# The sums of the gate weights in the second block, made by accumulating transfers begun on GpSimd

## What is computed

```python
h = rmsnorm_2(x, pre_norm_g[l])
proj = h @ w_in[l]
(u, v, z_a, c_q, c_kv, k_rope, z_b, x_c, z_c, g_a, g_b, g_c) = jnp.split(proj, cuts, axis=-1)
y_a = gmlp_spatial(u, v, ...) * silu(z_a)
y_b = mla_attention(c_q, c_kv, k_rope, ...) * silu(z_b)
y_c = rg_lru(x_c, ...) * silu(z_c)
merged = (sigmoid(g_a) * (y_a @ w_proj_a[l]) + sigmoid(g_b) * (y_b @ w_proj_b[l])
          + sigmoid(g_c) * (y_c @ w_proj_c[l]))
x = x + rmsnorm_2(merged @ w_out[l], post_norm_g[l])
```

## Time and profile before

| | |
|---|---|
| median of 3 runs | 3142.86 us (3142.70 to 3143.12) |
| profiled execution, its own time | 3142.73 us |
| its span, first to last instruction | 3141.4 us |
| PE busy | 3129.8 us, 100% of the span |
| PEld busy | 2644.8 us, 84% |
| DVE busy | 1953.5 us, 62% |
| ACT busy | 1316.9 us, 42% |
| POOL busy | 546.5 us, 17% |
| POOL's 64 additions for the sums (L2530) | 1.31 to 1.39 us each, 2.30 at most |
| moved by DMA | 353.71 MB, 113 GB/s |

### The profile page before, as it was taken

How to read it: one execution, slowest core, us unless ns; L and a number is a source line. 1 busy time by engine, 2 the same in 40 slices (tenths; PEclk the granted TensorE clock), 3 DMA queues, 4 the chain that set the end, 5 groups by cost and what they waited for, 6 DMA issues and landing times.

```text
span 3141.4 us, 38508 instructions
## 1 busy us (share of the span) xinstructions
PE 3129.8 (100%) x15416; PEld 2644.8 (84%) x15416; DVE 1953.5 (62%) x2640; ACT 1316.9 (42%) x2059; POOL 546.5 (17%) x395
## 2 busy tenths in 40 slices
PE   9999999999999999999999999999999999999999
PEld 8888888888888888888887888888888788888887
DVE  6876456565687655665558744457756764455774
ACT  4333334344433334343445532236745543233762
POOL 1201212110020111111013210130221321131031
PEclk9999999999999999999999999999999999999999
DMA  4322323235443233222652233223442222223423
GB/s 169 117 99 96 98 97 107 95 115 199 149 121 99 90 101 114 94 94 96 206 171 83 79 97 102 86 98 112 127 168 97 82 97 95 94 88 101 137 96 136
DMA packets 105906, 353.71 MB, mean 113 GB/s; under 512 B 13888, under 2 KB 14144, under 8 KB 104448
## 3 DMA queue, kind: packets, MB, share of 16 engines
q1 hardware_dynamic: 101856, 328.47, 32.0%
q0 software_dynamic: 3728, 22.25, 1.9%
q10 hardware_dynamic: 144, 0.52, 0.1%
HBM read 328.64 MB, written 6.29 MB: 107 GB/s over the span
## 4 chain that ended last, share of the span: by engine, by line
PE 95%; DVE 3%; ACT 1%; DMA 0%; SPq 0%; issue 0%; POOL 0%; POOLq 0%
PE ps L632 94%; DVE r L1750 1%; DVE wl L1740 1%; PE ps L723 1%; PE ps L1014 0%; DVE f L1755 0%; SPq L2666 0%; DVE f L1818 0%; DMA X<-x_in 0%; DMA f<-f 0%; DVE f L2053 0%; DVE r L2232 0%; ACT wh L1147 0%; ACT f L1560 0%; DVE sm L2258 0%; PE ps L676 0%
## 5 line engine op out<-in xcount | busy, mean ns | idle before, releaser
L632 PE MATMUL ps<-h,wh 128*128 128x512 f32 (+1 forms) x5696 | 1609.5, 368 | 0.7
L632 PEld LDWEIGHTS ps<-h,wh 128*128 128x128 f32 x5696 | 1029.8, 188 | 182.8 <-issue 3.4
L632 PE MATMUL ps<-h,wl 128*128 128x512 f32 (+1 forms) x2848 | 1046.1, 367 | 0.0
L1740 DVE TENSOR_TENSOR wl<-raw,wh 128x1024 fp32r<-128x1024 f32 (+2 forms) x551 | 681.9, 1248 | 265.3 <-ACT wh L1147 264.7
L1147 ACT CAST wh<-raw 128x1024 fp32r<-128x1024 f32 (+3 forms) x564 | 557.7, 1004 | 441.0 <-PE ps L632 436.7
L632 PEld LDWEIGHTS ps<-h,wl 128*128 128x128 f32 x2848 | 534.6, 188 | 88.6
L632 PE MATMUL ps<-r,wh 128*128 128x512 f32 x1536 | 474.8, 390 | 3.0 <-DVE f L2276 2.0
L632 PEld LDWEIGHTS ps<-r,wh 128*128 128x128 f32 x1536 | 284.6, 188 | 62.4 <-issue 2.9
L1244 ACT CAST r<-f 128x512 fp32r<-128x512 f32 x194 | 119.4, 622 | 511.5 <-DVE f L2151 149.0
L632 PE MATMUL ps<-r,wl 128*128 128x512 f32 x792 | 304.3, 389 | 0.0
L632 PE MATMUL ps<-wh,r 128*128 128x512 f32 x960 | 302.5, 390 | 0.2
(11 more groups left out here) (193 smaller groups left out, 2846.5 us busy)
## 6 DMA issues: line engine op xcount, KB each, us to landing
raw<-wst SPq DMA_DIRECT2D x544, 512.0 KB, 3.3
raw<-wst SPq DMA_DIRECT2D x48, 320.0 KB, 2.9
r<-r SPq DMA_DIRECT2D x64, 128.0 KB, 2.3
f<-gains POOLq DMA_DIRECT2D x6, 1024.0 KB, 5.2
raw<-wst SPq DMA_DIRECT2D x20, 256.0 KB, 2.9
f<-f SPq DMA_DIRECT2D x72, 64.0 KB, 2.0
f<-tab POOLq DMA_DIRECT2D x16, 256.0 KB, 5.0
kept_x<-X POOLq DMA_DIRECT2D x2, 2048.0 KB, 9.2
```

Source lines behind the costliest of these rows:

```text
L632: return e.matmul(o, a, b, start=start, stop=stop, skip_group_check=True)
L1740: e.tensor_tensor(l[:, 0:WIDTH[c]], sources(c)[0], h[:, 0:WIDTH[c]].bitcast(F32), ALU.subtract).then_inc(*lo_cut.up(("lo", c)))
```

## The change

POOL no longer adds. For each pair it begins six transfers of 256 KB instead, straight from `wst` in HBM:

- `sums_begin`: a plain one that brings one's first half to the buffer of sum 0, and a plain one that brings two's first half to the buffer of sum 2 (the "third").
- `sums`: when these have landed, an accumulating one each: two's first half onto the first buffer (it is now sum 0), two's second half onto the other (sum 2).
- `sums_more`: when DVE has split sum 0, an accumulating one of two's second half onto the same buffer (sum 1); when DVE has split sum 1, one of one's second half (sum 3).

Sums 0, 1 and 3 share one buffer. The four buffers now hold two pairs in turn (`sum_at`), and `sums_begin` of a pair waits for the splits of the pair before the last (`sums_free`). The raw buffers of a pair are released when quarter 1's and quarter 2's raw halves are split. In POOL's order the begins of both pairs of b stand at once ahead of `sums`, those of a and c stand one pair ahead of `sums`, the first of them behind all eight `a_prod` (a) or behind the last `add_gated` of a (c). In b the root of the first layer norm stands between `sums` and `sums_more` of the second pair. The programs of PE, ACT and DVE keep their order.

```diff
--- before.py
+++ after.py
@@ -216,18 +216,25 @@
     c = RAW_OF.index(r) if r in RAW_OF else RAW_OF.index(r - 1)
     if c not in PART:
         return (("lo", c),)
-    return ("sums", CHUNKS[c][0][:-2], 3), ("lo", c + 2)
+    return (("lo", c + 2 if r not in RAW_OF else c + 1, 0),)
 
 
 SUMS_AT = {"b": (64, 65, 66, 55), "a": (46, 47, 48, 54), "c": (31, 28, 29, 30)}
 
 
-def sums_free(name, q):
+def sum_at(name, q):
+
+    n = PAIR_J[name[6]].index(int(name[8])) % 2
+    return SUMS_AT[name[6]][n + 2 if q == 2 else n]
+
+
+def sums_free(name, third):
 
     L, nm, j = int(name[0]), name[6], int(name[8])
-    if j != PAIR_J[nm][0]:
-        return ("lo", NAME[f"{name[:8]}{j - 2}*{q}"])
-    c = ("done", ("ri", L, 9)) if q else ("done", ("pr", L, "a", 7))
+    n = PAIR_J[nm].index(j)
+    if n > 1:
+        return ("lo", NAME[f"{name[:8]}{PAIR_J[nm][n - 2]}*{2 if third else 3}"])
+    c = ("done", ("ri", L, 9)) if third or n else ("done", ("pr", L, "a", 7))
     return {"b": ("done", ("ob", L, 7)), "a": ("gated", L, "b", 7), "c": c}[nm]
 
 
@@ -544,7 +551,7 @@
             r, q = RAW_OF[c], PART.get(c)
             if q is None:
                 return [raw[:, r % NRAW, 0:WIDTH[c]]]
-            t = F(SUMS_AT[CHUNKS[c][0][6]][q])
+            t = F(sum_at(CHUNKS[c][0][:-2], q))
             return [raw[:, (r + q // 2) % NRAW, (S if q else 0):(2 * S if q else S)], t] if q < 3 else [t]
 
         def stat(t):
@@ -592,10 +599,11 @@
         pool_tile, pool_sum, pool_col = (Signal(sem(n)) for n in ("s_pool_tile", "s_pool_sum", "s_pool_col"))
         signals = [group_done, hi_cut, lo_cut, act_tile, act_hi, act_square, dve_tile, dve_lo, dve_tap,
                    dve_col, pool_tile, pool_sum, pool_col]
+        sum_done, third_done = ([Signal(sem(f"s_{what}{i}"), 16) for i in range(2)] for what in ("sum", "third"))
         swap_done = [Signal(sem(f"s_swap{r}"), 16) for r in range(5)]
         spread_done = {r: Signal(sem(f"s_spread{r}"), 16) for r in (0, 2)}
         far_done = [Signal(sem(f"s_far{t}"), 16) for t in range(5)]
-        signals += swap_done + list(spread_done.values()) + far_done
+        signals += sum_done + third_done + swap_done + list(spread_done.values()) + far_done
         loads = {}
 
         def landed(name):
@@ -2516,18 +2524,32 @@
                     roots(B, ("x", 2), ("y", 3))
                 roots(B, ("x", 3))
 
+            def sums_begin(name):
+
+                r, n = RAW_OF[NAME[f"{name}*0"]], PAIR_J[name[6]].index(int(name[8])) % 2
+                w.wait_ge(*at(*sums_free(name, False)))
+                e.dma_start(F(sum_at(name, 0)), wst[r, :, 0:S]).then_inc(*sum_done[n].up(("sum_begun", name)))
+                w.wait_ge(*at(*sums_free(name, True)))
+                e.dma_start(F(sum_at(name, 2)), wst[r + 1, :, 0:S]).then_inc(*third_done[n].up(("third_begun", name)))
+
             def sums(name):
 
-                r, t = RAW_OF[NAME[f"{name}*0"]], [F(i) for i in SUMS_AT[name[6]]]
-                one, two = raw[:, r % NRAW, :], raw[:, (r + 1) % NRAW, :]
-                w.wait_ge(s_raw[r % NRAW], 16 * (r // NRAW + 1))
-                w.wait_ge(s_raw[(r + 1) % NRAW], 16 * ((r + 1) // NRAW + 1))
-                for q, (a, b) in enumerate(((one[:, 0:S], two[:, 0:S]), (t[0], two[:, S:2 * S]), (two[:, 0:S], two[:, S:2 * S]),
-                                            (t[1], one[:, S:2 * S]))):
-                    w.wait_ge(*at(*sums_free(name, q)))
-                    if q in (1, 3):
-                        w.wait_ge(*at("sums", name, q // 2))
-                    e.tensor_tensor(t[q], a, b, ALU.add).then_inc(*pool_tile.up(("sums", name, q)))
+                c, n = NAME[f"{name}*0"], PAIR_J[name[6]].index(int(name[8])) % 2
+                r, t = RAW_OF[c], F(sum_at(name, 0))
+                w.wait_ge(*at("sum_begun", name))
+                e.dma_start(t, wst[r + 1, :, 0:S], accum_op=ALU.add).then_inc(*sum_done[n].up(("sums", name, 0)))
+                w.wait_ge(*at("third_begun", name))
+                e.dma_start(F(sum_at(name, 2)), wst[r + 1, :, S:2 * S], accum_op=ALU.add).then_inc(
+                    *third_done[n].up(("sums", name, 2)))
+
+            def sums_more(name):
+
+                c, n = NAME[f"{name}*0"], PAIR_J[name[6]].index(int(name[8])) % 2
+                r, t = RAW_OF[c], F(sum_at(name, 0))
+                w.wait_ge(*at("lo", c, 1))
+                e.dma_start(t, wst[r + 1, :, S:2 * S], accum_op=ALU.add).then_inc(*sum_done[n].up(("sums", name, 1)))
+                w.wait_ge(*at("lo", c + 1, 1))
+                e.dma_start(t, wst[r, :, S:2 * S], accum_op=ALU.add).then_inc(*sum_done[n].up(("sums", name, 3)))
 
             def save_rows(B):
 
@@ -2625,9 +2647,14 @@
                         *landed(f"ln{L - 2}{i}"))
                 for i in range(2):
                     e.dma_start(F(44 + i), gmb[L - 2, :, (4 + i) * S:(5 + i) * S]).then_inc(*landed(f"ws{L - 2}{i}"))
+                for j in PAIR_J["b"]:
+                    sums_begin(f"{L}/gateb_{j}")
                 sums(f"{L}/gateb_3")
+                sums_more(f"{L}/gateb_3")
                 sums(f"{L}/gateb_5")
-                for i in range(4):
+                small_step("layer_norm", L, 0)
+                sums_more(f"{L}/gateb_5")
+                for i in range(1, 4):
                     small_step("layer_norm", L, i)
                 for j in range(8):
                     q, q2 = F(49 + j % 3), F(52 + j % 2)
@@ -2635,8 +2662,12 @@
                     w.wait_ge(*at("za_silu", L, j))
                     e.tensor_tensor(q, q, q2, ALU.mult).then_inc(*pool_tile.up(("a_prod", L, j)))
                 for b in "ac":
+                    sums_begin(f"{L}/gate{b}_2")
                     for j in PAIR_J[b]:
+                        if j < 6:
+                            sums_begin(f"{L}/gate{b}_{j + 2}")
                         sums(f"{L}/gate{b}_{j}")
+                        sums_more(f"{L}/gate{b}_{j}")
                         if j > 2:
                             add_gated(L, b, (j - 4, j - 3))
                     add_gated(L, b, (4, 5, 6, 7))
```

## The result

The change made the kernel slower: 3221.56 us, median of 4 runs (3219.53 to 3225.07), against 3142.78 us of the kernel before on the same chip; the ratio is 1.0252, 95% interval 1.0234 to 1.0269. In a later comparison of more rounds it was 3223.86 against 3142.64 us, ratio 1.0261 [1.0247, 1.0275]. The forecast was 3189, with a range from 3163 to 3248. The profiled execution of after took 3225.07 us, 82.3 more than that of before. One of the 15 executions of the kernel before that stand beside x5 to x8 took 5328.84 us at a granted clock of 0.58; it is left out of all ratios, intervals and comparisons here.

What follows compares the result with a forecast made beforehand. TensorE was taken as the bound, so added waits count one to one. Per layer 11.2 + 0.3 + 4.5 + 3.7 + 3.5 = 23.2 us, 46.4 in two; 3142.7 + 46.4 = 3189 us, range 3163 to 3248.

Steps and rivals of the forecast that it cites:

- The bound: Whole kernel: TensorE busy 3129.8 of 3141.4 us, so every wait added on its path adds to the time one to one.
- The two facts: Each pair: u2 waits for p1's copy, mostly behind quarter 3's cast; sums 1 and 3 start behind splits of sums 0 and 1.
- The queue at a's first pair: Begins stand behind all eight a_prod products, first issued at 2025.6, 8.5 us ahead of u2; stall 11.2 us.
- L: Issue and landing of one accumulating transfer, in every pair: taken as 4.2 us, range 3.0 to 5.6.
- The link's own part: Each chained sum: cast 0.6, subtraction 0.7, wait and issue 0.1, in all 1.4 us beside the transfer.
- my formulas: Stalls by pair: a's first 3L - 1.4, b's second 2L - 8.1, c's second 2L - 4.7, third 2L - 4.9 us.
- the sign that I had named for L above 4.5: Waits of TensorE in a's later pairs and in b's would show L above 4.5; no size given.
- The waits: TensorE's stalls a layer: a's first pair 11.2, b's second 0.3, c's 4.5, 3.7, 3.5 us; 46.4 in two layers.
- The rival of the clock: TensorE's clock halves after the new waits: 3197 us from a's first pair, 3208 with c's too; chance 0.25.
- Slow transfers (L = 8): Rival, all pairs: accumulating transfers take 8 us, costing 79.2 us a layer, 3301 in all; chance 0.12.
- not slower: Rival: the chain fits into the lead in all pairs, 3141.5 us, decided at L = 1.4; chance 0.08.
- GpSimd's waits ahead of `add_gated`: Rival: split waits in GpSimd's queue delay `add_gated`, which frees a's gates; no cost at L = 4.2; no chance given.

Runs made afterwards that it cites:

- x5: Kernel after with all four accumulating transfers made plain, so the sums are not formed: 3185.7 us, ratio 1.0138.
- x8: Kernel before with GpSimd's four additions for a's first pair moved ahead of the last two a_prod products: 3141.11 us against 3142.24, ratio 0.9996.
- x4: Kernel after with GpSimd additions in place of the transfers, same chained order and queue places, no begins: 3145.64 us, ratio 1.0011.
- x3: Kernel after with ScalarE's copies of p1 and n5 ahead of the cast of quarter 3 in every pair: 3209.0 us.
- x6: Kernel after with sums 1 and 3 each made by two 128 KB adding transfers in series: 3312.5 us in one run.
- x2: Kernel after with begins of a's first two pairs ahead of the a_prod products, first adding transfers ahead of the last two: 3207.7 us.
- the filler: Kernel after with useless matmuls in TensorE's waits in a's first and c's last two pairs: 3218.57 us, later 3221.18 against 3223.86 without.

## Why the prediction was right or wrong

**The bound** was read rightly (one wait of before is 1.1 us and not at most 1.0, at the very start): every wait added to TensorE's path came into the time, and 27 us less of VectorE and 29 us less of GpSimd gave nothing back. x4 shows that the whole loss hangs on the transfers.

**The two facts.** u2 behind the cast of quarter 3: right, by x3. Sums chained behind splits, with the landing in each link: right, by the chain of waits, by x4 and by x6.

**The queue at a's first pair**: right. The whole trace is 1.1 us later here, from b; taken off, the first begin is at 2025.4 (forecast 2025.6) and the first adding transfer at 2029.0 (forecast 2028.9). x2 takes this away and wins 14 us.

**L, the term that failed first.** I took 4.2 for all. I called 3.0 us the price of a transfer that is alone; it was the first of a burst, but with no weight load beside it. Over all places the medians were near 4.2 (4.4 for sum 1, 4.2 for sum 3, 4.9 for sum 0), but in a's first pair, where L counts three times, it was 4.9, 5.3 and 6.5. The link's own part was 1.74 us (2042.05 to 2043.79) and not 1.4, since 0.4 lies between the end of the subtraction and the issue. Together u2 is 16.0 us late there (2051.22 - 1.1 - 2034.11) and not 11.2. Solved for L, my formulas give 5.8 in that pair, but 4.6 and 4.4 in c's last two, 4.5 in b, 4.9 in a's third (the sign that I had named for L above 4.5, a wait in b's and a's later pairs, came with 0.9 to 1.1 us). The mistake was one value for a sum whose largest term sits where other transfers run beside every link. Beside sum 0's transfer there are three more of GpSimd's own burst and no weight load. For sums 1 and 3, x2, with 5.5 and 6.7 us there after the burst of begins is gone, says that it is not that burst. The 512 KB weight loads are what is left, and the trace of the kernel after speaks for them. These are the rows for two adding transfers, sum 3 in a's first pair (2043.79 to 2050.25) and sum 1 in c's first (2264.97 to 2269.01); the queue of the weight loads, q1, has no row beside the second because it moved nothing there:

```profile
q1 hardware_dynamic: 144, 0.52, 22.8%
...
f<-wst POOLq DMA_DIRECT2D x1, 256.0 KB, 6.5
```
```profile
f<-wst POOLq DMA_DIRECT2D x1, 256.0 KB, 4.0
```

Of the 32 transfers for sums 1 and 3, the 13 beside which q1 moved 0.5 MB or more took 4.7 to 6.5 us, the 13 with 0.12 MB or less 3.6 to 4.1, the other six 3.8 to 5.3. A transfer that lasts longer also has more moved beside it, and no run took the loads away, so this is a strong correlation and not a test.

The prediction's two estimates from the Trainium skill (3.2 us from DMA: Bandwidth & Descriptors, section "Anatomy of one DMA — SWDGE (gpsimd) path"; 3.8 from Collectives: The Full Stack, section "The bandwidth ceiling") were both too low for the transfers of sums 3 and 1, 4.2 and 4.4 by the trace. The second page has an add slower for its two source reads; that adding is slower, the trace agrees, with 1.0 to 1.2 us for sums 1 and 3.

**The waits**: 57.3 us idle against 46.4, 10.9 more. Of the 5.5 a layer 2.4 lie in a's first pair (its u2 is 4.8 later than forecast, but half of that time TensorE was not idle, it ran n5 and p2 slowly), 0.9 in a's later pairs, 0.7 in b's and 0.5, 0.8 and 0.3 in c's.

**"TensorE's busy time should stay at 3130"**: wrong, it was 3154.3. The rival of the clock came true together with the forecast: 25.4 us of slow matmuls, nearly all in a's first pair and in c's three. I gave it 8 or 19 us and 0.25 of chance, as if it excluded the forecast; with waits of 8 us forecast beside a trace that had none over 1.1, it should have been a term of the sum, with its own bounds. The Trainium skill's rule (TensorE: Matmul & The Clock Gate, "Part 1: The HAM clock gate": idle lowers the clock, work brings it back) agrees with the trace, 0.50 after the waits and 1.00 from 2056. But the fallen clock is worth less time than its 25.4 us in the trace: where the filler kept it, some 3 us came back, since in a's second pair the next transfer was then late.

**Slow transfers (L = 8)** and **not slower** did not occur (no transfer of the chain took over 6.5 us); x4, with additions of 1.3 us as links, is at 3145.6, which is where the second had put the turning point (within 0.2% at L = 1.4). **GpSimd's waits ahead of `add_gated`**: nothing of TensorE's waits for that line appears.

Sum: 46.4 forecast, 10.9 more idle time, 25.4 of slow matmuls: 82.7, against 82.3 in the profiled executions. The range held the time because its upper end had the clock and L = 5.6 in it. So the places and the mechanism were right; the point forecast was not: it had 46 of the 79 us, with one term too small (L where three links stand in series) and one left out of the sum (the clock), and it is the width that covered both.

## What to carry to other kernels

A transfer that has to be waited for inside a chain of short steps costs its whole latency at each link, and little of that is its own bytes (half of them saved 1 us); it was long where weight loads ran beside it. Here 1.3 us of addition became 4 to 6.5 us, and freeing two engines that were not the bound paid for none of it. Before work is handed to transfers, count how many landings stand in series behind the last thing that releases them, and hold that against the lead; price the landing at the place where it counts most, beside the loads that run there. And when a forecast adds waits of several microseconds to TensorE, put its fallen clock into the sum, but expect part of it to hide behind the next wait. An engine made faster also starts the transfers behind it sooner: ask what they will run beside.

## What the runs showed of the hardware

- An adding transfer of 256 KB from HBM: its issue holds GpSimd for 0.87 to 0.93 us in the median, by line (0.54 plain), and a second one issued right behind another took up to 1.24; landing 3.6 to 8.8 us, medians 4.2 to 5.4 by line. For sums 1 and 3: 3.6 to 4.1 us with at most 0.12 MB of weight loads moving beside it, 4.7 to 6.5 with 0.5 MB or more.
- Half the bytes (128 KB, adding) landed in 3.1 and 3.4 us in the median: 1 us less than 256 KB.
- TensorE's clock after a wait: 1.00 after 0.85 us, 0.50 after 4.9 us. With plain transfers (x5) c's second pair of L=2 had one of 1.77 us, and the next stretch ran at 0.58:

```profile
2288.00:2292.00 4.00, 2.23 (x19) 1.00 0.22 72
2292.00:2296.00 4.00, 4.00 (x23) 0.58 0.89 301
```

  while in the same pair of L=3, after a wait of 1.79 us, it stayed at 1.00. So the length of the wait alone doesn't decide it.
- One execution of the changed kernel differs from the next far more than one of before (3219.5 to 3229.8 us against 3141.7 to 3143.3). Landings differ between them at the same place: sum 3 in a's first pair of L=2 took 6.5 us in one trace and 5.6 in the other, of L=3 5.4 and 6.5.
